# The scan of a recurrence's terms in three pieces, and the steps behind it one place later

## What is computed

```python
def rwkv_dir_terms(r, k0, v, wl, al, w0, w2, a0, a2, k_k, k_a, r_k):
    ...
    w_log = -jax.nn.softplus(-(w0 + jnp.tanh(wl) @ w2)) - 0.5
    decay = jnp.exp(-jnp.exp(w_log))
    a = jax.nn.sigmoid(a0 + al @ a2)
    ...
    k = hs(k0 * (1.0 + (a - 1.0) * k_a))
    ...
    bonus = jnp.sum(rh * k * r_k, axis=-1, keepdims=True) * vh

def rwkv7_scan(r, w, k, v, kk, bb, s0, reverse):
    def step(s, inp):
        r_t, w_t, k_t, v_t, kk_t, b_t = inp
        sa = jnp.einsum('bhij,bhj->bhi', s, kk_t)
        s = s * w_t[:, :, None, :] - sa[..., None] * b_t[:, :, None, :] + v_t[..., None] * k_t[:, :, None, :]
        return s, jnp.einsum('bhij,bhj->bhi', s, r_t)
```

## Time and profile before

| what | value |
|---|---|
| median of 3 runs | 3148.85 us (3147.89 to 3151.09) |
| the profiled execution, its own time | 3144.85 us |
| its span | 3143.1 us |
| TensorE (PE) busy | 2825.9 us, 90% |
| VectorE (DVE) busy | 1862.5 us, 59% |
| ScalarE (ACT) busy | 1153.1 us, 37% |
| GpSimd (POOL) busy | 1023.7 us, 33% |

### The profile page before, as it was taken

The page is one execution under the profiler, slowest core; times in us unless marked ns, Lnnn a source line. Parts: engine busy times, 40 slices in busy tenths (PEclk is TensorE's granted clock), DMA queues, the critical chain, the costliest instruction groups (busy, mean ns, idle before and its releaser), DMA issues. The chain is left out here.

```text
span 3143.1 us, 59081 instructions
## 1 busy us (share of the span) xinstructions
PE 2825.9 (90%) x25000; PEld 2232.2 (71%) x25000; DVE 1862.5 (59%) x2779; ACT 1153.1 (37%) x2127; POOL 1023.7 (33%) x582
## 2 busy tenths in 40 slices
PE   7999898999989998999999799978888887699987
PEld 5765576877867655777878587857777775479975
DVE  6888656885059786478840466466666654354062
ACT  4234434333242334343321422244454533242252
POOL 1422142444424221334443222244444430132202
PEclk9999899999999999999999899989999997899988
DMA  6321123433323211244332423210000003033111
GB/s 214 94 77 51 42 87 96 147 114 90 98 80 91 74 41 55 74 136 144 117 88 81 127 78 104 81 49 23 4 24 23 24 8 137 31 111 91 54 38 54
DMA packets 349911, 247.85 MB, mean 79 GB/s; under 512 B 10811, under 2 KB 322385, under 8 KB 349137
## 3 DMA queue, kind: packets, MB, share of 16 engines
q1 hardware_dynamic: 342384, 228.05, 24.0%
q10 hardware_dynamic: 7264, 16.03, 1.6%
HBM read 221.59 MB, written 16.52 MB: 76 GB/s over the span
## 5 line engine op out<-in xcount | busy, mean ns | idle before, releaser
L540 POOL TENSOR_TENSOR weights_lo<-weights_raw,weights_hi 128x1024 fp32r<-128x1024 f32 (+2 forms) x230 | 582.0, 2531 | 1111.3 <-ACT weights_hi L509 1111.3
L1181 PE MATMUL psum<-moving_hi,weights_hi 128*128 128x512 f32 x1472 | 601.7, 409 | 40.5 <-PEq L178 13.7
L1181 PE MATMUL psum<-moving_lo,weights_hi 128*128 128x512 f32 x1472 | 581.7, 395 | 0.0
L1181 PE MATMUL psum<-moving_hi,weights_lo 128*128 128x512 f32 x1472 | 581.2, 395 | 0.0
L1181 PEld LDWEIGHTS psum<-moving_hi,weights_hi 128*128 128x128 f32 x1472 | 281.0, 191 | 160.8 <-issue 67.8
L509 ACT ACTIVATE weights_hi<-weights_raw 128x1024 fp32r<-128x1024 f32 (+1 forms) x240 | 248.3, 1036 | 249.3 <-PE psum L1181 244.5
L1181 PEld LDWEIGHTS psum<-moving_hi,weights_lo 128*128 128x128 f32 x1472 | 281.0, 191 | 60.8
L1181 PEld LDWEIGHTS psum<-moving_lo,weights_hi 128*128 128x128 f32 x1472 | 282.2, 192 | 56.3 <-issue 3.8
L2585 POOL TENSOR_TENSOR second_off<-second_mats,second_masks 128x256 f32<-128x256 f32 x180 | 140.7, 786 | 157.4 <-PE psum L2061 156.7
L2641 PE MATMUL psum<-hn_hi,even_hi 128*128 128x256 f32 x480 | 166.4, 347 | 8.6 <-DVE hn_lo L1998 7.7
L2641 PE MATMUL psum<-hn_lo,even_hi 128*128 128x256 f32 x480 | 164.1, 342 | 0.0
(11 more groups left out here) (468 smaller groups left out, 6137.7 us busy)
## 6 DMA issues: line engine op xcount, KB each, us to landing
weights_raw<-in_w_up SPq DMA_DIRECT2D x88, 512.0 KB, 3.7
weights_raw<-in_w_in SPq DMA_DIRECT2D x80, 512.0 KB, 3.7
ada<-in_ada_w SPq DMA_DIRECT2D x9, 2048.0 KB, 9.4
odd_raw<-in_od_w_in SPq DMA_DIRECT2D x16, 1024.0 KB, 5.5
even_raw<-in_ev_w_in SPq DMA_DIRECT2D x30, 512.0 KB, 4.0
weights_raw<-in_w_down SPq DMA_DIRECT2D x32, 448.0 KB, 3.7
weights_raw<-in_w_o SPq DMA_DIRECT2D x16, 512.0 KB, 4.0
weights_raw<-in_w_down SPq DMA_DIRECT2D x16, 512.0 KB, 3.9
```

The costliest lines, as they stand in the source:

```text
L540: ops.tensor_tensor(self.ring.lo[i % n][:, a:b], self.ring.raw[:, t % self.ring.landing, a:b], self.ring.hi[i % n][:, a:b].bitcast(F32), A ...
L1181: return nc.tensor.matmul(to, (hi, lo)[which][:, at:at + P], moving(k)[part], start=start and k == 0 and i == 0, stop=stop and k == n_k - ...
```

## The change

The scan of phase 1 becomes three scans over 256 columns each, in VectorE's phases 1, 2 and 3. The pieces start at multiples of 64 tokens, where `reset` is zero, so each may start from 0. The sums go from phase 2 to phase 3, behind the last piece. The exponentials and k go from phase 3 to phase 4, the bonus input and kk from phase 4 to phase 5, the bonus product from phase 5 to 6, VectorE's bonus and GpSimd's product of r from phase 6 to 7. TensorE's norm product stays in phase 3, ScalarE's column of decays in phase 7, and phases 8 to 11 as they are.

```diff
                 ...
-                if phase == 5 and d == 1:
+                if phase == 6 and d == 1:
                     pe.wait_ge(self.a_ready, 1)
                     pe.wait_ge(self.bonus_in, 1)
                     project(self.region, common["head_sum"], cum[:, :]).then_inc(self.bonus_ready, 1)
                 ...
-                if phase == 3:
+                if phase == 4:
                     act.wait_ge(self.sums_ready, self.n_sums)
                     total = cum if d == 0 else e1
                 ...
-                if phase == 1:
+                if 1 <= phase < 4:
                     dve.wait_ge(self.sg_ready, 1)
-                    chain.then(V.tensor_tensor_scan(cum[:, :], reset[:, :], sg[:, :], 0.0, ALU.mult, ALU.add))
-                if phase == 2:
+                    third = slice((phase - 1) * CTX, phase * CTX)
+                    chain.then(V.tensor_tensor_scan(cum[:, third], reset[:, third], sg[:, third], 0.0, ALU.mult, ALU.add))
+                if phase == 3:
                 ...
-                if phase == 3:
+                if phase == 4:
                     dve.wait_ge(self.sums_ready, self.n_sums)
                     dve.wait_ge(self.a_ready, 1)
                     chain.then(V.tensor_scalar(self.k[:, :], a[:, :], col("k_a", p), omka[:, p:p + 1], ALU.mult, ALU.add))
                 ...
-                if phase == 4:
+                if phase == 5:
                     if d == 1:
                 ...
-                if phase == 6 and d == 1:
+                if phase == 7 and d == 1:
                     dve.wait_ge(self.bonus_ready, 1)
                     V.tensor_tensor(o, self.region, v, ALU.mult)
                 ...
             def pool(self, pool, phase):
-                if phase == 6:
+                if phase == 7:
                     if self.loads:
                         pool.wait_ge(self.rkv_landed, 16)
                     pool.wait_ge(self.exps_ready, 1)
```

## The result

The changed kernel takes 3162.13 us (median of 5 runs, 3158.77 to 3169.35), the kernel before in the same set 3147.89 (5 runs, 3143.49 to 3151.09): a ratio of 1.0050 [1.0039, 1.0061], that is +15.7 us [12.3, 19.2]. The prediction said 3165. The execution that the profiler recorded is the longest of the five, 3169.35 us with a span of 3167.5; so I read places from it, and sizes from timed runs.

What follows compares the result with a forecast made beforehand. TensorE's waits for VectorE's state and ScalarE's copy of p bound the passes. Odd passes 8.9, clock 1.2, even passes 6.7, first terms 0.3 and pass 0 0.3 make +17.4 us: 3165 forecast, range 3152 to 3176.

Steps and rivals of the forecast that it cites:

- The scan is worth nothing: VectorE's scan, 1.72 to 1.90 us in the last units: nobody waits for it, so cutting it gains nothing.
- the upper bound: Time of one 256-column scan piece: 0.71 us expected, 0.61 at least, 0.91 with twice the fixed part.
- Odd passes: Exponentials in round 3: u of chunk 3 loses its 1.71 wait, u of chunk 4 waits 3.49; net +1.78, five times 8.9.
- The clock: Pass 7, granted 1.00 before, pays for its longer wait with a lower TensorE clock too: 1.2 us added.
- nothing in the others: Clock term outside pass 7: no addition, because the other passes already pay for the lower clock.
- Even passes: p of chunk 4 -0.2, u of chunk 5 +0.43, y of round 7 +1.1: +1.3 per pass, five times 6.7.
- the 2.83 taken over from round 3: Even passes, round 5: time from the bonus input's start to the add's end, behind the 1.1 wait of y of round 7.
- the late product of r: Even passes: GpSimd's product of r, one round later, meets masks with some 0.6 to spare; costed at nothing.
- The small terms: Terms before pass 0 pay two fixed parts, 0.3 us; pass 0, without recurrence, is given +0.3.
- that rival's 3136: Faster rival: odd passes' exponentials are covered in round 3, giving back 1.71 and clock, -13.4 us; 9 in 100.
- The even passes don't pay for the odd ones: About-the-same rival, there claiming they do: no collision, bonus input hidden, -0.8 in five even passes, 3155; 12 in 100.
- The lock between the pieces: Slower rival: GpSimd masks get in between scan pieces in even passes, five times 0.8 later, 3170; 8 in 100.

Runs made afterwards that it cites:

- e1: Kernel before with the scan in three pieces, all at the scan's old place, nothing else moved: 3147.90 us, ratio 1.0000.
- e2: Kernel before with only the odd passes' three exponentials moved from round 1 to round 3: 3155.45 us, ratio 1.0024.
- e3: Changed kernel with the odd passes' exponentials put back in round 1: 3157.03 us, ratio 1.0029 to the kernel before.
- e4: Kernel before with the even passes' bonus steps one phase later, GpSimd's product of r left in place: 3156.64 us, ratio 1.0027.
- e12: Changed kernel's even passes and pass 0, with the odd passes of the kernel before: 3156.12 us, ratio 1.0025.
- e10: e5 with k of the even passes also moved from round 1 to round 3: 3144.40 us, ratio 0.9987 to the kernel before.
- e5: e4 with GpSimd's product of r also one phase later: 3141.60 us, ratio 0.9984 to the kernel before.
- e7: Kernel before, even passes: exponentials, k and bonus input cut up over several rounds, both sums one place earlier: 3119.02 us, ratio 0.9910.
- e9: e5 with the even passes' exponentials also moved from round 1 to round 3: 3158.72 us, ratio 1.0038 to the kernel before.
- e8: e7 plus the odd passes' exponentials cut up over rounds 1, 2 and 4: 3111.33 us, ratio 0.9882 to the kernel before.

## Why the prediction came out as it did

- **The scan is worth nothing: right.** e1 gives 0.0 us. A piece is a little longer than the 0.71 I worked out, 0.84 in the median of 36 (with the fixed part doubled my formula gives 0.81, not the 0.91 that I called the upper bound), as the row of its line in the changed kernel shows:

```profile
L2320 DVE TENSOR_TENSOR_SCAN second_cum<-second_reset,second_sg x36: 648/835/1036, 2061.9 to 2532.5; 128x256 f32<-128x256 f32 x36
```

- **Odd passes: right in place and nearly in size.** u of chunk 3 lost its 1.71; u of chunk 4 waits 3.31, forecast 3.49. Net 1.60 instead of 1.78. With the clock I had 10.1 us; the five odd passes of the profile are 9.8 longer, and e2, the exponentials alone, gives 7.6 [4.1, 11.0]. I hadn't seen that k in round 3 delays the outputs' addition (e3); it costs nothing only as long as ScalarE is later.
- **The clock.** Pass 7 fell from 1.00 to 0.92 and is 3.55 longer, 1.60 of it the wait, so 1.95 for the 1.2 I gave (the earlier trace rows would have given 42.16 - 40.68 = 1.48). But "nothing in the others" failed both ways: pass 3 fell from 0.96 to 0.92 too, and two even passes came to 1.00.
- **Even passes: the steps right in kind, the sum a little small.** p of chunk 4 comes 18.51 us into pass 10, and came 18.79 into pass 6 before: 0.28 earlier, forecast 0.2. p of chunk 5 follows 4.17 later, forecast 4.43; u of chunk 5 6.02 after p of chunk 4, forecast 5.92 (by the earlier trace rows the copy of u ends 1.58 after p, not 1.5). y of round 7 waits 1.48, forecast 1.1: the term that was mis-sized is the 2.83 taken over from round 3 as it stood there. In round 5 the bonus input's second instruction took 1.36, not 1.02, beside a mask that GpSimd had begun 0.44 earlier and the product of r. That the late product of r itself costs nothing held, but only because the change moves it along with the bonus input: left where it was it costs 1.07 a pass more (e4). Net +1.75 per pass (46.05 against 44.30), forecast +1.3: 8.8 us at full clock for 6.7, and e12, with pass 0, measured 7.9 [4.7, 11.0]. The one profile of the changed kernel shows only +2.4 over these five passes, because two of them ran at 1.00, and none of the profile before did.
- **The small terms.** The terms before pass 0 cost nothing (17.3 us in both), forecast 0.3. Pass 0 is 1.05 longer, forecast 0.3: at 2095.86 y waits 1.35 for GpSimd's masks, two of which took 2.49 beside k in round 3.
- **The rivals.** The exponentials are not covered in round 3 (3.31); that rival's 3136 had also left out the loss of the even passes. The even passes don't pay for the odd ones: alone they lose 7.9. The lock between the pieces, with p of chunk 4 some 0.6 later, did not come: the pieces take the collisions (2.07 for two), and the first sum is freed of them (0.96 for 1.26). The rule behind that rival, of the Trainium skill, SBUF — State Buffer, section "Who interferes with whom", agrees in kind all the same with what a longer GpSimd instruction did to VectorE: in e4 the bonus input's instruction took 1.42 more than alone, and had begun 1.63 before GpSimd's product ended.
- **One point on method.** The sum, 17.4, came within 2 us of the measured 15.7 with errors of both signs, so its closeness is in part luck: by the rows at full clock it was 2 too little in the even passes, and 0.75 in pass 0; by e2 it was 2.5 too much in the odd passes with their clock. That is inside what the timed runs can tell (3.4 either way).

## What to carry to other kernels

Where one engine's order is written out, a moved block is priced by the cover between the two instructions that its engine owes to that order, before and after the move: count what stands between them, not how busy the engine is. Waits lie over one another, so taking away one block may only uncover the next (e10, e3); take away those that end at the same place together. And before moving such a block to a later place, try to cut it, or look for an earlier place with cover: the exponentials and the bonus input in pieces between the copies and states that TensorE needs, with the sums one place earlier, gave 37 us, where moving all of it whole to a later place cost 16.

## What the runs showed of the hardware

- VectorE and GpSimd nearly took turns: in e4 2.44 for 1.02 us on VectorE and 2.52 for 1.81 (the same product's median in the kernel before) on GpSimd, over operands of 128x768. Which of the two started first decided how long VectorE took, and so how long TensorE waited at y of round 7, 2.56 in e4 and 1.49 in e5. Where VectorE's instruction began first and nothing of GpSimd's was running, it kept its time: in pass 8 of the changed kernel it began at 2455.95, 0.35 ahead of a mask, and took 1.02, and the mask 1.26 for 0.73. The move of one round was worth 13 us (e4 to e5), the clock included.
- The same waits went with different clocks. The wait of 1.71 at u of chunk 3 is in every odd pass of the kernel before, e4, e5, e7 and e9 to e12; of five such passes one was granted 1.00 in the kernel before, four in e4, two in e10, and three in each of the rest; the others had 0.96. In e8, where in passes 2 to 10 TensorE waits 0.95 at most, at a pass's start, the clock was 1.00 in all of them, and the passes got 11 us shorter than the 29 of the waits. What decides in between, these runs don't tell.
